# The feed-forward block as 2 x 2 block products with seven half products each

## The reference

```
x  = x + mix                                   # mix: output of the mLSTM/S5 part
hf = rmsnorm(x, g_ffn)                          # D_MODEL = 1024
x  = x + (silu(hf @ w_ff1) * (hf @ w_ff3)) @ w_ff2    # D_FF = 2816
y  = rmsnorm(x, g_final)
```

## Time and profile before

| | |
|---|---|
| median of three runs | 953.78 us |
| the profiled execution | span 952.6 us |
| TensorE busy | 939.6 us, 99% of the span, 8916 matmuls |
| VectorE / ScalarE / GpSimd busy | 531.5 / 439.3 / 205.1 us |
| feed-forward block | 560.9 to 943.4 us |

### The profile page before, as it was taken

The page is one execution under the profiler, slowest core; times in us unless marked ns, Lnnn a source line. Parts: engine busy times, 40 slices in busy tenths (PEclk is TensorE's granted clock), DMA queues, the critical chain, the costliest instruction groups (busy, mean ns, idle before and its releaser), DMA issues.

```text
span 952.6 us, 21457 instructions
## 1 busy us (share of the span) xinstructions
PE 939.6 (99%) x8916; PEld 908.4 (95%) x8916; DVE 531.5 (56%) x913; ACT 439.3 (46%) x725; POOL 205.1 (22%) x369
## 2 busy tenths in 40 slices
PE   8999999999999999999999999999999999999997
PEld 4899998999999999999999999999999999999997
DVE  6869985783684487643334655444444444333334
ACT  5469558729828858433323343343332432222221
POOL 6888868542722021000000000000000000000000
PEclk9999999999999999999999999999999999999998
DMA  8523155172253343632332323323223332333312
GB/s 299 174 79 122 46 185 205 67 286 82 101 217 121 109 151 129 213 126 92 111 111 90 92 86 99 99 80 99 88 88 88 92 98 96 89 95 106 95 60 90
DMA packets 28077, 113.23 MB, mean 119 GB/s; under 512 B 3524, under 2 KB 5620, under 8 KB 26088
## 3 DMA queue, kind: packets, MB, share of 16 engines
q1 hardware_dynamic: 23616, 81.22, 26.9%
q0 software_dynamic: 2736, 24.13, 6.8%
q10 hardware_dynamic: 1656, 6.89, 2.0%
HBM read 98.83 MB, written 13.39 MB: 118 GB/s over the span
## 4 chain that ended last, share of the span: by engine, by line
PE 83%; POOL 7%; DVE 5%; issue 2%; ACT 2%; DMA 0%; ACTq 0%; DVEq 0%; SPq 0%; POOLq 0%
PE G L1610 67%; PE G L1700 4%; PE Q L1610 3%; POOL pool_tmp L815 3%; PE G L1971 2%; DVE c_samples L1349 1%; PE Q L1758 1%; PE Q L1768 1%; POOL c_abar_packed L818 1%; PE G L1811 1%; POOL u_by_step L975 1%; PE Q L1732 1%; PE Q L1841 1%; DVE x_scaled L1166 1%; DMA x_tokens<-xt 0%
## 5 line engine op out<-in xcount | busy, mean ns | idle before, releaser
L454 ACT ACTIVATE w_high<-raw 128x1024 fp32r<-128x1024 f32 x146 | 154.1, 1059 | 287.7 <-PE G L1610 272.4
L1082 DVE TENSOR_TENSOR w_low<-raw,w_high 128x1024 fp32r<-128x1024 f32 x146 | 181.3, 1245 | 172.1 <-ACT w_high L454 171.5
L1610 PE MATMUL G<-h_high,w_high 128*128 128x256 f32 x1344 | 272.7, 284 | 0.0
L1610 PE MATMUL G<-h_low,w_high 128*128 128x256 f32 x1344 | 270.8, 283 | 0.0
L1610 PE MATMUL G<-h_high,w_low 128*128 128x256 f32 x1344 | 270.7, 283 | 0.0
L1610 PEld LDWEIGHTS G<-h_high,w_high 128*128 128x128 f32 x1344 | 208.4, 188 | 2.1 <-issue 1.6
L1610 PEld LDWEIGHTS G<-h_low,w_high 128*128 128x128 f32 x1344 | 208.4, 188 | 0.0
L1610 PEld LDWEIGHTS G<-h_high,w_low 128*128 128x128 f32 x1344 | 208.3, 188 | 0.0
L1610 PE MATMUL G<-hidden_low,w_high 128*128 128x256 f32 (+1 forms) x308 | 62.0, 283 | 0.0
L1610 PE MATMUL G<-hidden_high,w_high 128*128 128x256 f32 (+1 forms) x308 | 62.0, 283 | 0.0
L1610 PE MATMUL G<-hidden_high,w_low 128*128 128x256 f32 (+1 forms) x308 | 61.7, 281 | 0.0
(11 more groups left out here) (403 smaller groups left out, 1585.9 us busy)
## 6 DMA issues: line engine op xcount, KB each, us to landing
raw<-wst SPq DMA_DIRECT2D x147, 512.0 KB, 3.6
c_samples<-c POOLq DMA_DIRECT2D x4, 2048.0 KB, 8.9
out_cs<-c_samples POOLq DMA_DIRECT2D x4, 2048.0 KB, 8.0
v_spread<-v_scratch ACTq DMA_DIRECT2D x4, 1024.0 KB, 5.1
x_tokens<-xt SPq DMA_DIRECT2D x4, 520.0 KB, 4.9
x_residual<-xt POOLq DMA_DIRECT2D x1, 2080.0 KB, 9.0
small<-small ACTq DMA_DIRECT2D x1, 1785.0 KB, 7.8
heads_scratch<-head_h POOLq DMA_DIRECT2D x3, 520.0 KB, 3.0
```

What stands on the lines that cost most here:

```text
L454: return act.activation(out, in_, ACT.Copy, **kw)
L1082: tt(WL[n.slot()][:], raw[n.slot()][:], WH[n.slot()][:].bitcast(F32), ALU.subtract).then_inc(w_lo, 1)
L1610: last = mm(o, w[slot][:, c], h[:, k, c0_:c0_ + width], start=start and x == 0 and t == 0, stop=stop and x == n - 1 and t == 2)
```

## The change

For the pair of products of the up projection and for the down projection, the kernel computes 2 x 2 block products with seven block products in place of eight (Winograd's form of Strassen's scheme). The blocks of a round: rows are two pairs of output tiles, the contraction is split in two (4 + 4 input tiles in an up round; 4 + 4, 4 + 4 or 3 + 3 hidden tiles in a down round), and the tokens in two halves of 260.

- The hidden tiles are made in three groups of 8, 8 and 6 (`DOWN_CUT`). Each group has 4, 4 or 3 up rounds and two down rounds, in this order (`ROUNDS`, 17 rounds): up up up up down down, up up up up down down, up up up down down. An up round makes four hidden half-tile columns (2 row tiles x 2 halves, for both factors at once: the gate in G, the other factor in Q); a down round makes four output tiles.
- Seven weight blocks are used per round: A11, A12 and A22 as loaded and four sums of blocks, `F = A21 + A22`, `F - A11`, `A22 - F`, `A12 - F`. GpSimd forms the sums (`sum_up`), each once its operands' low parts are made. Each product i of a round has its weight block as a unit: high part by ScalarE (`split_high`), low part by VectorE (`split_low`), in a ring of four slots. A unit is 2 x 512 numbers per partition (2 x 384 in the third group's down rounds).
- Seven input blocks: BH, BL for x1, HIDH, HIDL for the hidden tiles. GpSimd makes the differences of x1's blocks, VectorE those of the hidden ones.
- Product i runs as two halves, `su` = 0 into G and 1 into Q, of k x 3 matmuls of 260 columns. Product 0 and 5 use bank 2, product 2 bank 1, products 1, 3, 4 and 6 bank x (0 or 3, by turns). Products that follow in a bank and do not belong to its sum wait until the earlier one is taken out: 3 for `took_x1`, 4 for `took_x3`, 5 for `took_z0`, 6 for `took_x4`.
- In an up round ScalarE takes products 0, 1, 3 and 4 out, VectorE adds 2 and 5 and takes 6. In a down round VectorE adds all seven into X1, and its low part for the unit four ahead (`next_low`) stands in front of each take.
- ScalarE begins the next up round with a wait for the hidden low parts of the last one. The first down round of a group runs products 0 to 2 without their last pair of tiles, then waits for these.
- The feed-forward part is written out without loops. The final norm is computed for halves of 260; GpSimd scales tiles 5 to 7 of each half, VectorE tiles 0 to 4.

```diff
-DOWN_CUT = (0, 8, 15, 22)
+DOWN_CUT = (0, 8, 16, 22)
...
+HALF = T // 2
+PAIRS_OF = tuple((b - a) // 2 for a, b in zip(DOWN_CUT, DOWN_CUT[1:]))
+ROUNDS = tuple(r for g, n in enumerate(PAIRS_OF) for r in [("up", g, p) for p in range(n)] + [("down", g, p) for p in range(2)])
+NR = len(ROUNDS)
+UNITS_R = 7
+RHS = (2, 0, 6, 4, 3, 1, 5)
...
+        def bank_x(r):
+            return 0 if r % 2 == 0 else 3
...
+            for r in range(1, NR):
+                before = N_FF + UNITS_R * (r - 1)
+                if r == 1:
+                    sp.wait_ge(w_lo, N_FF)
+                else:
+                    sp.wait_ge(w_lo, before - UNITS_R + 6)
+                load_a21(r)
+                if r >= 2:
+                    sp.wait_ge(w_lo, before - UNITS_R + 7)
+                load_a22(r)
+                sp.wait_ge(w_lo, before + 5)
+                load_a11(r)
+                sp.wait_ge(sums, 4 * (r - 1) + 4)
+                load_a12(r)
...
+            def split_high(q):
+                r, i = divmod(q, UNITS_R)
+                if q >= 4:
+                    act.wait_ge(su_done, 2 * (q - 4) + 2)
+                if i == 0 or 3 <= i < 6:
+                    act.wait_ge(sums, 4 * r + (1, 0, 0, 2, 3, 4)[i])
+                elif i == 1:
+                    act.wait_ge(a11_in, 16 * r + 16)
+                elif i == 2:
+                    act.wait_ge(a12_in, 16 * r + 16)
+                else:
+                    act.wait_ge(a22_in[r % 2], 16 * (r // 2) + 16)
+                copy(halves_of(WH[w_at(q)], r), halves_of(round_source(r, i), r)).then_inc(w_hi, 1)
...
+            def up_round(r):
+                u, x, k = up_index(r), bank_x(r), hid_at(r)
+                def take(i, bank, slot, s):
+                    for su, (t, o) in enumerate(((G, DT[:, slot, :]), (Q, CB[:, min(slot, 3), :]))):
+                        act.wait_ge(su_done, 2 * (UNITS_R * r + i) + su + 1)
+                        copy(o, t[:, bank, 0:HALF]).then_inc(s, 1)
+                def next_high(i):
+                    if UNITS_R * r + i + 4 < UNITS_R * NR:
+                        split_high(UNITS_R * r + i + 4)
+                if u > 0:
+                    act.wait_ge(hidl_ready, 2 * u - 1)
+                take(0, 2, 2, took_z0)
+                next_high(0)
+                take(1, x, 1, took_x1)
+                next_high(1)
+                next_high(2)
...
+                take(3, x, 0, took_x3)
+                next_high(3)
+                if u > 0:
+                    act.wait_ge(hidl_ready, 2 * u)
+                take(4, x, 7, took_x4)
+                next_high(4)
+                next_high(5)
+                act.wait_ge(a_early, u + 1)
+                act.activation(DT[:, 0:3, :], DT[:, 0:3, :], ACT.Silu).then_inc(silu_done, 1)
+                act.wait_ge(took_x6, 2 * r + 1)
+                act.activation(DT[:, 7, :], DT[:, 7, :], ACT.Silu).then_inc(silu_done, 1)
+                next_high(6)
+                act.wait_ge(hid_ready, 2 * u + 1)
+                copy(HIDH[:, 0:5, k, :], DT[:, 1:6, :]).then_inc(hidh_ready, 1)
+                act.wait_ge(hid_ready, 2 * u + 2)
+                copy(HIDH[:, 5:7, k, :], DT[:, 6:8, :]).then_inc(hidh_ready, 1)
...
+            def sum_up(r, step):
+                f, b, d, e = (halves_of(x, r) for x in (FB[r % 2], BB, DB, EB[r % 2]))
+                unit = N_FF + UNITS_R * r
+                if step == 0:
+                    pool.wait_ge(a21_in[r % 2], 16 * (r // 2) + 16)
+                    pool.wait_ge(a22_in[r % 2], 16 * (r // 2) + 16)
+                    tt(f, f, e, ALU.add).then_inc(sums, 1)
+                elif step == 1:
+                    pool.wait_ge(a11_in, 16 * r + 16)
+                    pool.wait_ge(w_lo, unit + 1)
+                    tt(f, f, b, ALU.subtract).then_inc(sums, 1)
+                elif step == 2:
+                    pool.wait_ge(sums, 4 * r + 2)
+                    pool.wait_ge(w_lo, unit + 2)
+                    tt(b, e, f, ALU.subtract).then_inc(sums, 1)
+                else:
+                    pool.wait_ge(sums, 4 * r + 3)
+                    pool.wait_ge(a12_in, 16 * r + 16)
+                    pool.wait_ge(w_lo, unit + 4)
+                    tt(f, d, f, ALU.subtract).then_inc(sums, 1)
...
+                sum_up(r, 2)
+                sum_up(r, 3)
+                if r < NR - 1:
+                    sum_up(r + 1, 0)
+                    sum_up(r + 1, 1)
+                if kind == "up":
+                    for su, (p5, u3) in enumerate(((DT[:, 2, :], DT[:, 7, :]), (CB[:, 2, :], CB[:, 3, :]))):
+                        pool.wait_ge(took_z0, 2 * r + su + 1)
+                        pool.wait_ge(took_x4, 2 * r + su + 1)
+                        tt(p5, p5, u3, ALU.add).then_inc(c22_ready, 1)
+                    if u == 0:
+                        pool.wait_ge(inverse_ready, 3)
+                    pool.wait_ge(c22_ready, 2 * u + 2)
+                    pool.wait_ge(took_y2, 2 * r + 2)
+                    pool.wait_ge(took_z5, 2 * r + 2)
+                    tt(CB[:, 0:3, :], CB[:, 0:3, :], frq[:, 0:3, :], ALU.mult).then_inc(b_early, 1)
...
+                pool.wait_ge(inverse_copied, count + 1)
+                for m in range(5, KC):
+                    own.do(tt(X1[:, m, (H0, H1)[half]], X1[:, m, (H0, H1)[half]], inv_sb[:, half, :], ALU.mult))
+                    pool.tensor_scalar(X1[:, m, (H0, H1)[half]], X1[:, m, (H0, H1)[half]], g_fin[:, m:m + 1], None, ALU.mult).then_inc(y_pool, 1)
...
+            def up_round(r):
+                u, x, k = up_index(r), bank_x(r), hid_at(r)
+                C = (DT, CB)
+                next_low(r, 0)
+                next_low(r, 1)
+                next_low(r, 2)
+                for su, t in enumerate((G, Q)):
+                    product_done(r, 2, su)
+                    dve.wait_ge(took_x1, 2 * r + su + 1)
+                    tt(C[su][:, 1, :], t[:, 1, 0:HALF], C[su][:, 1, :], ALU.add).then_inc(took_y2, 1)
...
+                next_low(r, 3)
+                next_low(r, 4)
+                next_low(r, 5)
+                for su, t in enumerate((G, Q)):
+                    product_done(r, 5, su)
+                    dve.wait_ge(took_x3, 2 * r + su + 1)
+                    tt(C[su][:, 0, :], t[:, 2, 0:HALF], C[su][:, 0, :], ALU.add).then_inc(took_z5, 1)
+                dve.wait_ge(c22_ready, 2 * u + 1)
+                dve.wait_ge(took_y2, 2 * r + 1)
+                dve.wait_ge(took_z5, 2 * r + 1)
+                tt(DT[:, 0:3, :], DT[:, 0:3, :], frq[:, 0:3, :], ALU.mult).then_inc(a_early, 1)
+                product_done(r, 6, 0)
+                tt(DT[:, 7, :], G[:, x, 0:HALF], frq[:, 3, :], ALU.mult).then_inc(took_x6, 1)
+                product_done(r, 6, 1)
+                dve.wait_ge(c22_ready, 2 * u + 2)
+                tt(CB[:, 3, :], Q[:, x, 0:HALF], frq[:, 3, :], ALU.mult).then_inc(took_x6, 1)
+                dve.wait_ge(silu_done, 2 * u + 1)
+                dve.wait_ge(b_early, u + 1)
+                own.do(tt(DT[:, 0:3, :], DT[:, 0:3, :], CB[:, 0:3, :], ALU.mult))
+                own.do(tt(DT[:, 3:5, :], DT[:, 0:3:2, :], DT[:, 1::-1, :], ALU.subtract))
+                tt(DT[:, 5, :], DT[:, 2, :], DT[:, 3, :], ALU.subtract).then_inc(hid_ready, 1)
+                dve.wait_ge(silu_done, 2 * u + 2)
+                dve.wait_ge(took_x6, 2 * r + 2)
+                own.do(tt(DT[:, 7, :], DT[:, 7, :], CB[:, 3, :], ALU.mult))
+                dve.wait_ge(hid_ready, 2 * u + 1)
+                tt(DT[:, 6, :], DT[:, 7, :], DT[:, 5, :], ALU.subtract).then_inc(hid_ready, 1)
+                next_low(r, 6)
+                dve.wait_ge(hidh_ready, 2 * u + 1)
+                tt(HIDL[:, 0:5, k, :], DT[:, 1:6, :], HIDH[:, 0:5, k, :].bitcast(F32), ALU.subtract).then_inc(hidl_ready, 1)
+                dve.wait_ge(hidh_ready, 2 * u + 2)
+                tt(HIDL[:, 5:7, k, :], DT[:, 6:8, :], HIDH[:, 5:7, k, :].bitcast(F32), ALU.subtract).then_inc(hidl_ready, 1)
...
+            def down_round(r):
+                x, p = bank_x(r), hid_at(r)
+                last = r == NR - 1
+                def take(i, bank, row, half, s, after=None):
+                    next_low(r, i)
+                    for su, t in enumerate((G, Q)):
+                        product_done(r, i, su)
+                        if after is not None:
+                            dve.wait_ge(after, 2 * r + su + 1)
+                        part = X1[:, 2 * p + feature(su, row), half]
+                        tt(part, part, t[:, bank, 0:HALF], ALU.add).then_inc(s, 1)
+                        if last and i >= 5:
+                            dve.wait_ge(s, 2 * r + su + 1)
+                            tt(sqh[2 * i - 6 + su][:], part, part, ALU.mult).then_inc(x2_late, 1)
+                        if last and i == 6 and su == 0:
+                            invert(1)
+                take(0, 2, 1, H1, took_z0)
+                take(1, x, 0, H0, took_x1)
+                take(2, 1, 0, H0, took_y2, took_x1)
```

(73 more changed lines are left out.)

499 lines of the change are left out of this document (281 added, 218 removed).

## The result

The changed kernel takes 1045.49 us in the median (1044.21 to 1047.1, four runs) against 954.45 us (953.16 to 955.2, four runs) before: ratio 1.096, 95% interval 1.0943 to 1.0976. Forecast were 960.6 us and 941 to 980. The direction was right; the size lies far outside the range. The profiled span grew from 952.6 to 1044.1 us, by 91.5.

What follows compares the result with a forecast made beforehand. TensorE's matmuls were taken to bound the kernel. Matmuls removed -47.5, undisturbed waits +41.9, GpSimd's contention +7.4 and the end +5 gave +6.8 us on the 952.6 us span; with the median's 1.2 above it, 960.6 us, range 941 to 980.

Steps and rivals of the forecast that it cites:

- Waits, undisturbed: New waits of TensorE in the feed-forward block's rounds, with every duration undisturbed; 41.9 us in all.
- (a): Down rounds, before product 4: TensorE waits for VectorE's take of product 3, queued behind a low part; 14.0 us.
- (c): Up round after up round, before product 3: hidden low parts hold ScalarE up; 1.4 us eight times, 11.2 us.
- (d): Down round after up round, three times: products 0 to 2 wait for the hidden low parts; 6.6 us.
- the start: Block's start: blocks of x1 that come late are needed only at product 3 or 4, 8.6 us on; 0.
- GpSimd beside VectorE: In the rounds, GpSimd's work slows VectorE's steps reading two SBUF tensors by a fifth; 7.4 us, bounds 0 and 15.
- rival 2: In the block, TensorE's clock falls after its long gaps; 16 us more, 977 us; chance 0.13.
- Its own signs: Forecast wrong if low parts stay at 1.22 us, gaps lie before product 0, or granted clock leaves 1.00.
- Rival 3: In up rounds, GpSimd becomes the bound if its sums take 3.5 us each; 20 us, 981 us; chance 0.10.
- Rival 1: At an up round's head, hidden blocks come in time: (c) vanishes, (d) shrinks; 941 us; chance 0.22.
- End: After the last matmul: GpSimd's three of eight tiles per half finish later; +5 us, bounds +1 and +7.
- (b): Same chain as (a) with one product in between, such as product 1 to 3; mostly covered, 1.0 us.

Runs made afterwards that it cites:

- small sums: Changed kernel with GpSimd's four weight sums a round covering 8 of 1024 numbers per partition, all instructions and waits kept: 983.1 us.
- one_input: Changed kernel with GpSimd's weight sums replaced by scalings of one tile, one operand read in place of two: 1013.3 us.
- fill: Changed kernel with useless matmuls added on TensorE where it stood still, ahead of product 3 or 4 of certain rounds: 1037.5 us.
- both: Changed kernel with small sums and, in down rounds, VectorE's take put ahead of the next low part: 954.8 us.
- pieces: Changed kernel with each GpSimd weight sum made as four instructions of 256 columns in place of one of 1024: 1047.5 us.

## Why the prediction was wrong

**What bounds the kernel, and the matmuls removed:** right. 2772 at 0.12 are the 332.9 us that lie between the gaps.

**Waits, undisturbed:** right in place and mechanism, short in size. (a) came at 14.9 for 14.0 in the kernel after and at 14.5 with small sums. With small sums and the order kept or mended, (c) was 1.8 for 1.4 and (d) 7.6 for 6.6. Missing was the start, which I had put down at 0 because I asked when GpSimd's blocks are needed and not when VectorE, whose queue waits for them, frees the bank of product 1: 5.5 and 3.3 us in the kernel after, 4.4 with small sums. In all the gaps with small sums are 50.5 us for 41.9.

**GpSimd beside VectorE:** this step failed. It stood at 7.4 us with bounds of 0 and 15; the runs say 62.4 (after to small_sums), with the low clock that it brings and the length of the sums themselves. Two errors. I read the mean of 1.42 against 1.22 as a rate, and it is a mixture: of the seven low parts two took 1.21 and 1.22 us, with no instruction of GpSimd running at their start, and the other five 1.42 to 1.76. And I took 1.4 times as the upper bound, though a lock is bounded by the other engine's longest instruction: 2.40 us here, so a step of 0.95 took 3.1. The rows bore it. The low part of 1.72 began with 0.64 us left of a GpSimd instruction and took 0.50 longer; the product of 1.65 began with 1.11 left of the first of the two that the earlier trace rows show at 111.80, and took 0.96 longer. In a round up three of VectorE's steps met it at full length (3.09, 2.85, 3.40 in the timeline): 6.5 us of excess in VectorE's queue, which bounds the round at 26.6, against 22.2 with small sums, where VectorE is busy for 48.5 of 66.6 us and no longer the bound.
The Trainium skill (SBUF — State Buffer, "Who interferes with whom") says that a VectorE instruction with two inputs in SBUF and a GpSimd instruction that reads SBUF exclude each other, and that the second to issue blocks fully. The trace agrees for two operands on both sides: 3.09 us for 0.95. It differs where GpSimd reads one operand: there the step took 1.81 and ended 0.9 us ahead of GpSimd's instruction (one_input), and the measurement decides. The prediction went by the Trainium skill's line on contention (GPSIMD Engine Reference, section 1), which gives no size, and had not followed it to this rule.

**Clock (rival 2, 16 us):** came beside the forecast, not in place of it; that the sum has it at nothing is the second term that failed. In the kernel after it is worth some 8 us (fill). With GpSimd's load gone it is worth more: from small sums to both, which differ by 28.3 us, 16.5 are gaps (50.5 and 34.0) and some 12 come behind them; the mean granted clock of the block is 0.96 in the one (some 34 us at the lower level) and 0.99 in the other, that of the rounds down 0.94 and 1.00. Rival 2's 16 us was about right in size there. Its matmul of 0.217 us at 1.2 GHz is what the trace after shows, 0.21 to 0.22 between two starts.

**Its own signs:** two of the three signs that would prove the forecast wrong came, the clock and gaps ahead of product 0. The second had another cause than the late weights named for it: product 0 waits for VectorE's take of product 5.

**Rival 3 (GpSimd the bound, 981):** wrong for the reason given (its sums took 2.40, not 3.5), though GpSimd was late at the start of the block (3.3 us) and in pieces and one_input, where VectorE holds it up.

**Rival 1 (hidden blocks in time, 941):** refuted even at undisturbed lengths: (c) is 1.8, not 0, in the kernel with both edits.

**End:** +5 forecast, +5.9 measured, by the six pairs of 0.73 and 0.94 us on GpSimd, last in the chain.

Of the miss of 84.9 us, 55.0 is GpSimd's term (62.4 for 7.4). The other 29.9 remain with small sums, 983.1 against the 953.2 of a forecast without that term: 8.6 in gaps, 1.8 in a later start and a longer end, and some 19 in the low clock and the small matmuls of the block, which no run parts exactly. With the better order as well the kernel is at 954.8, by 28.3 less; the prediction knew of this order, and had 15 of the 28.3 as (a) and (b).

## What to carry to other kernels

Before work moves to GpSimd, list VectorE's instructions with two operands in SBUF on the critical chain, and charge each with up to a whole GpSimd instruction, not with a share; in this kernel the sums cost less on the fuller engine (1.22 us each) than on the idle one (2.40, and up to 2.2 of VectorE's time with them). In a queue, put what another engine waits for ahead of what prepares the next step. And a low clock is dear only in the stretches in which TensorE is the bound: compare stretch by stretch before pricing it.
